# One kernel, one change: a norm's two parts taken per k-tile straight from PSUM, with another order between the layers

## What is computed

```python
def rmsnorm(x, g):
    xf = x.astype(jnp.float32)
    xf = xf * lax.rsqrt(jnp.mean(xf * xf, axis=-1, keepdims=True) + EPS)
    return (xf * g.astype(jnp.float32)).astype(x.dtype)
...
    for i in range(DEPTH):
        h = h + 0.5 * swiglu(rmsnorm(h, ffn1_norm[i]), ffn1_w_gate[i], ffn1_w_up[i], ffn1_w_down[i])
        z = rmsnorm(h, mix_norm[i]) @ w_in[i]
...
        h = h + y @ w_out[i]
        h = h + 0.5 * swiglu(rmsnorm(h, ffn2_norm[i]), ffn2_w_gate[i], ffn2_w_up[i], ffn2_w_down[i])
        gate = jax.nn.sigmoid(rmsnorm(h, ple_norm[i]) @ ple_w_gate[i])
        h = h + (p[i] @ ple_w_proj[i]) * gate
    return rmsnorm(h, final_norm)
```

## Time and profile before

| | |
|---|---|
| median of 3 runs (lowest to highest) | 1000.63 us (1000.57 to 1000.84) |
| span of the profiled execution | 998.1 us |
| PE matmul busy | 984.3 us, 99% |
| DVE busy | 854.5 us, 86% |
| ACT busy | 515.9 us, 52% |
| POOL busy | 370.8 us, 37% |
| mean DMA rate | 182 GB/s |

### The profile page before, as it was taken

How to read it: one execution, slowest core, us unless ns; L and a number is a source line. 1 busy time by engine, 2 the same in 40 slices (tenths; PEclk the granted TensorE clock), 3 DMA queues, 4 the chain that set the end, 5 groups by cost and what they waited for, 6 DMA issues and landing times.

```text
span 998.1 us, 16112 instructions
## 1 busy us (share of the span) xinstructions
PE 984.3 (99%) x5553; PEld 832.7 (83%) x5553; DVE 854.5 (86%) x1400; ACT 515.9 (52%) x728; POOL 370.8 (37%) x577
## 2 busy tenths in 40 slices
PE   9999999999999999999999999999999999999996
PEld 7788878899978888888877888888998788888885
DVE  6898999889879888996789978997998888787865
ACT  5444344585754444444555444445856454444453
POOL 6888999910137888980008600001002000000000
PEclk9999999999999999999999999999999999999999
DMA  9766556533546846464635565645344664655541
GB/s 291 218 210 209 169 171 207 169 128 128 183 158 201 262 151 227 155 223 169 211 127 177 195 217 168 210 168 169 128 169 139 199 210 165 214 179 199 200 159 43
DMA packets 143600, 181.63 MB, mean 182 GB/s; under 512 B 18432, under 2 KB 125632, under 8 KB 143552
## 3 DMA queue, kind: packets, MB, share of 16 engines
q1 hardware_dynamic: 142312, 179.65, 54.2%
q10 hardware_dynamic: 1240, 1.36, 0.4%
HBM read 179.93 MB, written 1.05 MB: 181 GB/s over the span
## 4 chain that ended last, share of the span: by engine, by line
PE 90%; DVE 6%; issue 2%; ACT 1%; DMA 0%; POOL 0%; POOLq 0%; DVEq 0%
PE ps L1539 29%; PE ps L1541 28%; PE ps L1540 28%; DVE hTf L930 2%; DVE wL L829 2%; PE ps L1554 2%; PE ps L1826 1%; PE ps L1792 1%; ACT wH L447 0%; PE ps L1856 0%; PE ps L1850 0%; PE ps L1836 0%; DVE uL L856 0%; DMA ctmp<-in_ffn_norm_dram 0%; DVE xres L870 0%
## 5 line engine op out<-in xcount | busy, mean ns | idle before, releaser
L829 DVE TENSOR_TENSOR wL<-raw,wH 128x1024 fp32r<-128x1024 f32 x334 | 421.6, 1308 | 23.9 <-ACT wH L447 22.8
L447 ACT ACTIVATE wH<-raw 128x1024 fp32r<-128x1024 f32 x334 | 334.1, 1050 | 81.9 <-PE ps L1541 80.4
L1539 PE MATMUL ps<-wH,uH 128*128 128x512 f32 x832 | 326.4, 392 | 1.7 <-DVE wL L829 1.2
L1541 PE MATMUL ps<-wH,uL 128*128 128x512 f32 x832 | 324.0, 389 | 0.0
L1540 PE MATMUL ps<-wL,uH 128*128 128x512 f32 x832 | 323.9, 389 | 0.0
L930 DVE STREAM_TRANSPOSE hTf<-bufB 32x128 f32<-32x128 f32 x640 | 193.8, 303 | 9.5
L1539 PEld LDWEIGHTS ps<-wH,uH 128*128 128x128 f32 x832 | 156.2, 188 | 36.7 <-DVE uL L856 3.0
L1541 PEld LDWEIGHTS ps<-wH,uL 128*128 128x128 f32 x832 | 156.2, 188 | 32.9
L1540 PEld LDWEIGHTS ps<-wL,uH 128*128 128x128 f32 x832 | 156.3, 188 | 31.4
L1539 PE MATMUL ps<-wH,hTH 128*128 128x512 f32 x352 | 138.2, 393 | 0.8 <-DVE wL L829 0.8
L1541 PE MATMUL ps<-wH,hTL 128*128 128x512 f32 x352 | 137.1, 390 | 0.0
(11 more groups left out here) (198 smaller groups left out, 1065.9 us busy)
## 6 DMA issues: line engine op xcount, KB each, us to landing
raw<-in_ffn_w_down_dram SPq DMA_DIRECT2D x88, 512.0 KB, 4.0
raw<-in_ffn_w_gate_dram SPq DMA_DIRECT2D x86, 512.0 KB, 4.0
raw<-in_ffn_w_up_dram SPq DMA_DIRECT2D x86, 512.0 KB, 5.0
raw<-in_w_in_dram SPq DMA_DIRECT2D x32, 512.0 KB, 4.4
raw<-in_w_out_dram SPq DMA_DIRECT2D x16, 512.0 KB, 3.8
raw<-in_ple_w_gate_dram SPq DMA_DIRECT2D x16, 512.0 KB, 4.1
raw<-in_glu_w_dram SPq DMA_DIRECT2D x4, 512.0 KB, 3.7
raw<-in_ple_w_proj_dram SPq DMA_DIRECT2D x4, 512.0 KB, 3.8
```

The costliest lines, as they stand in the source:

```text
L447: nc.scalar.activation(wH[:, slot, w], raw[:, slot, w], ACT.Copy).then_inc(wh_done, 1)
L829: nc.vector.tensor_tensor(wL[:, slot, w], raw[:, slot, w], wH[:, slot, w].bitcast(F32), ALU.subtract).then_inc((wl_half, wl_done)[a], 1)
L1539: mul(o, sH, vH, start=start, stop=False)
L1541: return mul(o, sL, vH, start=False, stop=stop)
```

## The change

`tg`, its semaphore and `gained` go. `norm_H` is four activations of 128x128, each from the turned quarter in PSUM with one column of gains as its scale. `rest` is four multiply-subtracts of 128x128 from the same PSUM bank. Both count per k-tile (`u_at`), and where a norm's first product begins PE waits for each k-tile ahead of its matmuls. Waits on `tg_done` become waits on `ul_done`. `turn_tile0` puts both quarters of tile 0 behind item 5 (m = 1, 2) or item 7 (m = 3), where they stood behind items 4 and 5 or 5 and 6. Between the layers the transposes of tile 0 stay apart, behind items 4 and 5. There ACT runs norm quarter 0, the tanh of quarter 2, norm quarter 1, the tanh of quarter 3, and only then the second half of the split; DVE runs both products and additions of tile 1 ahead of tile 1's low parts; PE turns quarter 3 one k-tile earlier. A scratch buffer `tsq` takes the place of `tg` in two squares that have nothing to do with the norms.

```diff
         x_ready = sem("x_ready")
-        xt_ps, tg_done, uh_done, ul_done = sem("xt_ps"), sem("tg_done"), sem("uh_done"), sem("ul_done")
+        xt_ps, uh_done, ul_done = sem("xt_ps"), sem("uh_done"), sem("ul_done")
         ssq_done, rs_done = sem("ssq_done"), sem("rs_done")
...
             return l * 3 + (1, None, 2, 3)[m]
+
+        def u_at(l, m, q, k):
+
+            return l * 64 + 16 * m + 4 * q + k + 1
...
                 act.wait_ge(x_ready, DEPTH * 16 + 16 + q + 1)
                 nc.scalar.activation(squared, xres[:, q // 2, (q % 2) * 512:(q % 2) * 512 + 512].rearrange("p (i n) -> p i n", i=2),
...
-                t, h, turn = q // 2, q % 2, q
-                act.wait_ge(tg_done, l * 16 + (4 * m + turn + 1))
-                nc.scalar.activation(uH[:, 4 * h:4 * h + 4, t * P:(t + 1) * P],
-                                     tg[:, turn % 2, :].rearrange("p (k n) -> p k n", k=4),
-                                     ACT.Copy).then_inc(uh_done, 1)
+                t, h = q // 2, q % 2
+                act.wait_ge(pvt_done, l + 1) if l + m else act.wait_ge(pvt0_done, 1)
+                act.wait_ge(xt_ps, l * 16 + (4 * m + q + 1))
+                for k in range(4):
+                    g = V_NORM[m] + 4 * h + k
+                    nc.scalar.activation(uH[:, 4 * h + k, t * P:(t + 1) * P], ps[:, 2 + q, k * P:(k + 1) * P],
+                                         ACT.Copy, scale=pvT[:, l, g:g + 1]).then_inc(uh_done, 1)
...
                     E_turned(l, 1, 2)
-                act.wait_ge(ul_done, l * 16 + 8)
                 act.wait_ge(rsb_done, l * 2 + 1)
...
                 if l + 1 < DEPTH:
-                    def tile0_and_gate():
+                    def tile0_and_gates():
                         norm_H(l + 1, 0, 0)
+                        gate(2)
                         norm_H(l + 1, 0, 1)
-                        gate(2)
-
-                    split_at(l + 1, 1, tile0_and_gate)
-                    gate(3)
+                        gate(3)
+
+                    def tile1():
+                        squares(l + 1, 0, 1)
+                        norm_H(l + 1, 0, 3)
+
+                    split_at(l + 1, 1, tile0_and_gates)
                     squares(l + 1, 0, 0)
-                    split_at(l + 1, 2, lambda: norm_H(l + 1, 0, 2))
-                    squares(l + 1, 0, 1)
-                    norm_H(l + 1, 0, 3)
+                    norm_H(l + 1, 0, 2)
+                    split_at(l + 1, 2, tile1)
                 else:
...
-            def gained(l, m, q):
-
-                h, turn = q % 2, q
-                dve.wait_ge(xt_ps, l * 16 + (4 * m + q + 1))
-                if turn >= 2:
-                    dve.wait_ge(ul_done, l * 16 + (4 * m + turn - 1))
-                g = pvT[:, l, V_NORM[m] + 4 * h:V_NORM[m] + 4 * h + 4].unsqueeze(2).to_broadcast([P, 4, P])
-                nc.vector.tensor_tensor(tg[:, turn % 2, :].rearrange("p (k n) -> p k n", k=4),
-                                        ps[:, 2 + q, :].rearrange("p (k n) -> p k n", k=4), g,
-                                        ALU.mult).then_inc(tg_done, 1)
-
             def rest(l, m, q):
-                t, h, turn = q // 2, q % 2, q
-                dve.wait_ge(uh_done, l * 16 + (4 * m + turn + 1))
-                at = (slice(None), slice(4 * h, 4 * h + 4), slice(t * P, (t + 1) * P))
-                nc.vector.tensor_tensor(uL[at], tg[:, turn % 2, :].rearrange("p (k n) -> p k n", k=4),
-                                        uH[at].bitcast(F32), ALU.subtract).then_inc(ul_done, 1)
+                t, h = q // 2, q % 2
+                dve.wait_ge(uh_done, u_at(l, m, q, 3))
+                for k in range(4):
+                    g = V_NORM[m] + 4 * h + k
+                    at = (slice(None), 4 * h + k, slice(t * P, (t + 1) * P))
+                    nc.vector.scalar_tensor_tensor(uL[at], ps[:, 2 + q, k * P:(k + 1) * P], pvT[:, l, g:g + 1],
+                                                   uH[at].bitcast(F32), ALU.mult, ALU.subtract).then_inc(ul_done, 1)
             def half_norm(l, m, t):
-                for step in (gained, rest):
-                    for h in range(2):
-                        step(l, m, 2 * t + h)
+                for h in range(2):
+                    rest(l, m, 2 * t + h)
...
                 dve.wait_ge(pvt_done, l + 1)
-                gained(l, 1, 0)
-                gained(l, 1, 1)
                 rest(l, 1, 0)
...
                     half_split(n, 1, 1, 1)
-                    gained(n, 0, 2)
                     gated(3)
+                    added(3)
                     rest(n, 0, 2)
-                    added(3)
-                    gained(n, 0, 3)
                     rest(n, 0, 3)
...
                 dve.wait_ge(pvt0_done, 1)
-                gained(0, 0, 0)
-                gained(0, 0, 1)
                 rest(0, 0, 0)
...
                 rest(0, 0, 1)
-                gained(0, 0, 2)
-                gained(0, 0, 3)
                 rest(0, 0, 2)
...
                 base = FFN_BASE[f]
-                last_quarter = {1: lambda: turn_x(l, 0, 3)} if f == 0 else {}
+                last_quarter = {0: lambda: turn_x(l, 0, 3)} if f == 0 else {}
                 for t in range(NT):
                     for part in range(2):
-                        pe.wait_ge(ul_done, l * 16 + (8 * f + 2 * t + part + 1))
+
+                        def ready(k, t=t, part=part):
+                            if t == 1 and part == 0 and k in last_quarter:
+                                last_quarter[k]()
+                            pe.wait_ge(ul_done, u_at(l, 2 * f, 2 * t + part, k))
+                            if t == 0 and k == 2:
+                                take(l, base + part)
+
                         if t == 0:
                             pe.wait_ge(wl_half, l * UNITS + (base + part + 1))
-                        gate_up_tile((base + part) % SLOTS, part, t,
-                                     {2: lambda n=base + part: take(l, n)} if t == 0 else last_quarter if part == 0 else {})
+                        gate_up_tile((base + part) % SLOTS, part, t, {k: lambda k=k, ready=ready: ready(k) for k in range(4)})
                         if t == 0 and part == 0:
...
                     for t in range(NT):
-                        pe.wait_ge(ul_done, 2 * t + part + 1)
+                        weights = (unit0, unit1)[part] if t == 0 else {}
+
+                        def ready(k, t=t, part=part, weights=weights):
+                            pe.wait_ge(ul_done, u_at(0, 0, 2 * t + part, k))
+                            if k in weights:
+                                weights[k]()
+
                         if t == 0 and part == 0:
...
                             pe.wait_ge(wl_half, 2)
-                        gate_up_tile(part, part, t, (unit0, unit1)[part] if t == 0 else {})
+                        gate_up_tile(part, part, t, {k: lambda k=k, ready=ready: ready(k) for k in range(4)})
                     if part == 0:
...
-                q0 = 4 if m in (1, 2) else 5
-                return {q0: lambda: turn_x(l, m, 0), q0 + 1: lambda: turn_x(l, m, 1)}
+                return {5 if m in (1, 2) else 7: lambda: (turn_x(l, m, 0), turn_x(l, m, 1))}
...
                         pe.wait_ge(bc_ld, (l + 1) * (16 * NBC))
-                        pe.wait_ge(tg_done, l * 16 + 4)
+                        pe.wait_ge(ul_done, u_at(l, 0, 3, 3))
                     for q in range(4):
...
                 r = wL[:, n % SLOTS, :].rearrange("p (k c) -> p k c", k=KD)
-                if j == 0:
-                    pe.wait_ge(ul_done, l * 16 + 8)
                 if j < 2:
...
                     for k in range(KD):
+                        if j == 0 and i == 0:
+                            pe.wait_ge(ul_done, u_at(l, 1, 2 + k // 4, k % 4))
                         if (i, k) in beside:
...
                 elif r == 1:
-                    pe.wait_ge(tg_done, l * 16 + 8)
-                elif b == 2:
-                    pe.wait_ge(tg_done, l * 16 + 6)
+                    pe.wait_ge(ul_done, u_at(l, 1, 3, 3))
+                elif b >= 2:
+                    pe.wait_ge(ul_done, u_at(l, 1, b - 2, 3))
                 for j in range(4):
...
-                pe.wait_ge(tg_done, l * 16 + 8)
+                pe.wait_ge(ul_done, u_at(l, 1, 3, 3))
                 pe.wait_ge(diag_done, l * 2 + 2)
...
                       between=lambda: (turn_x(l, 3, 2), turn_x(l, 3, 3)))
-                pe.wait_ge(ul_done, l * 16 + 14)
-                rows2(l, U_GATE, uH, uL, 0, ACC, True, False, between=lambda: pe.wait_ge(ul_done, l * 16 + 16))
+                pe.wait_ge(ul_done, u_at(l, 3, 1, 3))
+                rows2(l, U_GATE, uH, uL, 0, ACC, True, False, between=lambda: pe.wait_ge(ul_done, u_at(l, 3, 3, 3)))
                 rows2(l, U_GATE + 1, uH, uL, 2, ACC, False, False)
...
```

More of the change, by code:

```diff
@@ L120, in trunk @@
         uL = sb("uL", [P, KD, SEQ], F32R)
-        tg = sb("tg", [P, 2, 512])
+        tsq = sb("tsq", [P, 512])
```

(4 more changed lines are left out.)

## The result

The changed kernel takes **1005.78 us** (median of 4 runs, 1004.71 to 1006.61) against 1000.60 for the kernel before in the same comparison (1000.18 to 1000.84): a ratio of 1.0052, 95% interval 1.004 to 1.0064. It is slower by 5.2 us, where 2.4 were forecast. The four times lie in two pairs, 1004.7 and 1005.1 with a mean granted clock of 0.997, 1006.5 and 1006.6 with 0.996; the profiled execution is of the upper pair, with a span of 1004.8, 6.7 above that of before. Two single traces overstate the difference here: in all four executions the device time is 1.8 above the span, so the profiled execution of before took about 999.9 (an estimate, 998.1 plus 1.8), 0.7 under its median, and that of the changed kernel lies 0.8 over its own.

The account below looks back on a forecast made before the run. PE, busy 984.3 of 998.1 us, was taken as the bound, so only waits could change. Gate +2.3, between layers +1.8, mixer -1.3, second FFN -0.2, start -0.2 gave +2.4, 1003.0 us (chance 0.54 for 1002 to 1004); range 1000.2 to 1005.2.

Parts of the forecast that it names:

- Cost of the small operations: Each norm quarter: ACT's scaled copies and DVE's multiply-subtracts, 128x128, would each start one every 0.25 us.
- (b): Rival: small operations slow on both engines, 0.29 on ACT and 0.32 on DVE; +6.1, 1006.7 us; chance 0.12.
- (c): Rival: only ACT's small operations slow, 0.29 us each; +3.9, 1004.5 us; chance 0.12.
- (d): Rival: not slower, the small operations hide, no wait at the gate; -1.7, 998.9 us; chance 0.09.
- Before the gate: Embedding's gate, both layers: transposes moved behind item 7 make PE wait 0.94 for tile 1's x; +1.15 each, +2.3.
- Between the layers: Once: tanh ahead of norm quarter 1 and DVE's eight low parts delay tile 1's x; +1.8 us.
- Wait at 538 stays: PE's later wait of 0.7 us for DVE at 538.05 stays, as DVE starts behind PE's delayed matmuls.
- (e): Rival: the stall between layers is swallowed, PE's 0.7 wait at 538.05 goes; +1.7, 1002.3 us; chance 0.13.
- Into the mixer: Both layers: PE's waits of 0.27 for x and 0.36 for low parts go; -0.63 each, -1.3.
- Into the second FFN: Both layers: waits of 0.42 and 0.16 go, but the weight split's first half ends later; -0.1 each, -0.2.
- Start: Once: ACT's first quarter is slower, low parts end 0.26 later, but the 0.44 wait at 12.95 goes; -0.2.
- Behind the last matmul: End of the kernel: no term in the prediction, which assumed that what lies outside the span stays.

Follow-up runs that it names:

- e0: The changed kernel run once more, unaltered; no time of its own is stated, its profiled execution had the 2.7 us wait and no clock fall.
- e3: Changed kernel with norm quarter 1 again ahead of the tanh between layers and the gate's transposes behind items 5 and 6: 1000.26 us, ratio 1.0002.
- e13: e3 with DVE's product and addition of quarter 2 ahead of the half split, plus 32 unused semaphore increments on DVE: 998.97 us, ratio 0.9988.
- e5: Kernel before, old wide parts, with the transposes ahead of the embedding's gate both behind item 7: 1001.41 us, ratio 1.0013.
- e6: Kernel before, old wide parts, with ACT running the tanh ahead of norm quarter 1 between the layers: 1001.50 us, ratio 1.0011.

## Why the prediction was wrong

The direction and the two main terms were right; the range, 1000.2 to 1005.2, missed the median by 0.6. The steps that failed are two costs that stood in no term: the stretch behind the last matmul, +0.94 in every execution, and PE's clock behind the long wait, +1.5 in some. Some 0.9 of small gains did not come besides. It took both missing costs to leave the range: without the 0.94 the median is 1004.8, and the executions without the fall lie at 1004.4 to 1005.1. Chance had a part too, since two of the first four executions had the fall; the median of all nine, 1005.0, lies inside. That does not mend the mechanism, which lacked both.

- **Cost of the small operations**: right. 0.25 forecast for both paces, 0.257 and 0.26 measured; rivals (b), (c) and (d), which were made of other paces, are out, although (c)'s 1004.5 lies nearer to the result than my 1003.0; its slow copies did not occur. (The terms of (b) add up to +6.0, not +6.1.) The Trainium skill's estimate of 0.293 ("ScalarE: Activation LUTs", "What ACT_TABLE_LOAD costs") is above the trace, which decides.
- **Before the gate**: right. +1.15 each forecast, +1.25 each measured; the wait 0.94 against 0.89.
- **Between the layers**: the mechanism was right, the size near without the clock, +1.95 against +1.8 (e0); PE turned the quarter 5.39 behind the tanh's start where I had 5.37. The step that failed is the one after it: I let PE wait 2.4 us and priced its next matmuls at full clock. The fall costs 1.5 in the executions that have it, and is in the profiled one.
- **Wait at 538 stays**: right; it grew by 0.1. Rival (e) is out.
- **Into the mixer**: mis-sized, -0.4 each against -0.63. Both waits went, as forecast (no wait at the first transposes or at the first w_in matmul); 0.25 comes back inside w_in, at the products that spread the row scale (line 1802), which I had in no term. They need two scale products of ACT (line 516 now, 510 before), and ACT the row scale from POOL, which starts from ACT's squares of tile 1. Those end at 200.83 instead of 200.40, behind ACT's eight copies. The changed kernel first, then before:

```profile
202.22 1.43 POOL L1469 TENSOR_TENSOR rs<-ms,mhalf 128x1 f32<-128x1 f32 x1
...
203.06 1.02 ACT L516 ACTIVATE bufA<-ident,rs 128x128 f32<-128x128 f32 x2
...
204.22 0.68 PE L1802 MATMUL ps<-bufA,ones 128*128 128x128 f32 x4
```

```profile
201.36 1.42 POOL L1479 TENSOR_TENSOR rs<-ms,mhalf 128x1 f32<-128x1 f32 x1
...
202.69 0.70 ACT L510 ACTIVATE bufA<-ident,rs 128x128 f32<-128x128 f32 x2
...
204.22 0.60 PE L1801 MATMUL ps<-bufA,ones 128*128 128x128 f32 x4
```

  ACT's second product starts at 203.68, just behind POOL's row scale, and ends at 204.08 instead of 203.38; PE's idle time before the product is 0.2. This chain is read from the trace, no run tried it.
- **Into the second FFN**: -0.1 forecast, 0.0 measured; as forecast PE's wait on x turned into one on the first half of the weight split (0.3 by the profile).
- **Start**: -0.2 forecast, 0.0 at the first FFN's end. The wait at 12.95 went. But the start differs from trace to trace of the same code: the wait on weights ahead of the first matmul is 0 to 1.2 in the four traces with the old parts and 0.5 to 1.6 in the thirteen with the new (1.2 in the profiled one), and that at 128 is 0.6 in the trace of before, 1.0 to 1.1 in the other three with the old parts and 0.8 to 1.3 in those with the new. A difference of some tenths between two single traces, the +0.5 at 128 too, can therefore not be put down to the change.
- **Behind the last matmul**: no term. I assumed that what lies outside the span stays, but the way from the last matmul to the span's end is inside it and went unpriced: +0.94, from the length of DVE's program alone.

In the profiled execution: 0.0 at the start, +0.5 at 128, -0.4 mixer, 0.0 second FFN, +1.25 gate, +3.4 between the layers, +0.1 at 538, and in layer 1 -0.4, 0.0 and +1.25, make 5.7 of the measured 5.8; with the tail 6.7.

## What to carry to other kernels

Replacing one wide operation by four narrow ones is paid where two engines hand over on the critical path, and whether it is paid there depends on what stands in front of the hand-over in each engine's queue: the same parts cost 5 us in one order, nothing in e3's, and stand 1.1 below the kernel before in e13, where a product is moved ahead and the last code fetch too. About half of the 5 us was no matter of width at all: the new places alone, with the old wide parts, cost 1.3 (e5) and 1.3 (e6). When a forecast contains a new wait of PE of the size seen here (2.7 us), price the clock behind it too, and see whether something, even something useless, can fill it. When the number of instructions of an engine changes, look for code fetches behind the last store: here the length of a queue that the bound never waited for decided over 0.94 us.

## What was not expected of the hardware

- An 8 KB fetch of code at the very end, which itself takes 0.31 us, delays the landing of the last store by 0.94 us, though the store's issue had ended 1.7 us before it; moved 18 us ahead it costs nothing. It was the same in each of thirteen traces with it.
- The granted clock fell to 0.50 behind 2.7 us without a matmul in 11 of 19 executions of three kernels (by their mean clock; two of the falls were profiled), for 3.4 us (507.9 to 511.3 in both), once 0.2 before PE was back and once 1.1 after; it did not in the other 8; behind 1.5 us (e6, 11 executions at 0.997 to 0.999) it never did.
- Idle PE filled with 22 transposes of the identity, into a bank that is overwritten, kept the clock from falling in all 16 executions (1.00 from 502 to 511 in the two profiled, a mean of 0.997 or 0.998 in all).
